# Down product over five PSUM banks, and the S5 matrices loaded where their buffer comes free

## The reference

```python
h = rmsnorm(x, norm_mix);  z = h @ w_in            # 1024 -> 3 x 512: xl, gl, us
hl = rglru(conv(xl));      y_lru = hl * gelu(gl)   # linear recurrence over tokens
ys = s5(us);               g = gelu(ys)            # diagonal complex state space, 32 groups
y_ssm = g * sigmoid(g @ w_glu + b)
x = x + concat(rmsnorm(y_lru), rmsnorm(y_ssm)) @ w_out
h2 = rmsnorm(x, norm_ffn)
ff = silu(h2 @ w_gate) * (h2 @ w_up)               # 1024 -> 2816
x = x + ff @ w_down                                # 2816 -> 1024
y = rmsnorm(x, norm_final)
```

## Time and profile before

| | |
|---|---|
| three runs | 2308.42, 2310.72, 2311.23 us; median 2310.72 |
| the profiled execution | 2311.55 us, of which the span from first to last instruction is 2309.8 |
| TensorE matmul | busy 2214.1 us, 96% of the span, 11582 instructions |
| VectorE, ScalarE, GpSimd | busy 1496.5, 1064.6 and 353.0 us (65%, 46%, 15%) |
| mean granted TensorE clock | 0.985 |
| DMA | 324.52 MB moved, 45.8% share of the 16 engines |

### The profile page before, as it was taken

One profiled execution on the slowest core, in us unless ns is written; L12 is line 12 of the kernel. 1 busy time (PEld: TensorE's weight loads), 2 busy tenths in 40 slices (PEclk: granted clock), 3 DMA queues, 4 the chain that ended last, 5 costly groups with the idle time before them and its releaser, 6 DMA issues.

```text
span 2309.8 us, 30129 instructions
## 1 busy us (share of the span) xinstructions
PE 2214.1 (96%) x11582; PEld 2094.1 (91%) x11582; DVE 1496.5 (65%) x2536; ACT 1064.6 (46%) x1432; POOL 353.0 (15%) x428
## 2 busy tenths in 40 slices
PE   6898889999999999999999999999999999999997
PEld 3565889999999999999999999999999999999996
DVE  8555555687666647875666677666658875665544
ACT  4325532564543455554434664543455464432232
POOL 4022200022101102311110132101102321100001
PEclk8999999999999999999999999999999999999998
DMA  6865233545334454543353655334455643343331
GB/s 209 206 205 158 87 106 118 135 161 170 110 119 148 140 141 160 181 126 120 118 169 119 167 169 172 110 119 148 139 141 160 168 129 111 117 149 110 120 125 60
DMA packets 201759, 324.52 MB, mean 140 GB/s; under 512 B 89296, under 2 KB 132944, under 8 KB 201488
## 3 DMA queue, kind: packets, MB, share of 16 engines
q1 hardware_dynamic: 201488, 322.36, 45.8%
q0 software_dynamic: 128, 0.23, 0.0%
HBM read 298.09 MB, written 26.53 MB: 141 GB/s over the span
## 4 chain that ended last, share of the span: by engine, by line
PE 86%; DVE 7%; ACT 3%; issue 2%; POOL 1%; DMA 1%; SPq 0%; POOLq 0%; DVEq 0%; ACTq 0%
PE acc L920 25%; PE acc L922 25%; PE acc L921 24%; PE acc L993 6%; DVE rstd L1207 1%; POOL tmp L629 1%; PE acc L1024 1%; PE acc L1015 1%; PE acc L1004 1%; PE acc L1014 1%; DVE w_hl L1090 1%; DVE act_hl L1090 1%; PE acc L986 1%; DVE x_acc L1090 0%; DVE s5prod L1090 0%
## 5 line engine op out<-in xcount | busy, mean ns | idle before, releaser
L920 PE MATMUL acc<-act_hl,w_hl 128*128 128x416 f32 x2448 | 877.4, 358 | 10.7 <-DVE act_hl L1090 9.7
L921 PE MATMUL acc<-act_hl,w_hl 128*128 128x416 f32 x2448 | 857.5, 350 | 0.0
L922 PE MATMUL acc<-act_hl,w_hl 128*128 128x416 f32 x2448 | 857.2, 350 | 0.0
L1090 DVE TENSOR_TENSOR w_hl<-w_raw,w_hl 128x1024 fp32r<-128x1024 f32 x416 | 513.4, 1249 | 74.8 <-ACT w_hl L716 73.5
L920 PEld LDWEIGHTS acc<-act_hl,w_hl 128*128 128x128 f32 x2448 | 463.0, 189 | 23.5 <-issue 10.9
L921 PEld LDWEIGHTS acc<-act_hl,w_hl 128*128 128x128 f32 x2448 | 463.7, 189 | 5.7 <-issue 4.8
L922 PEld LDWEIGHTS acc<-act_hl,w_hl 128*128 128x128 f32 x2448 | 462.6, 189 | 2.0
L716 ACT ACTIVATE w_hl<-w_raw 128x1024 fp32r<-128x1024 f32 x416 | 430.5, 1051 | 46.2 <-DMA w_raw<-in_w_ffn 24.1
L1090 DVE TENSOR_TENSOR x_acc<-x_acc,acc 128x416 f32<-128x416 f32 x480 | 272.2, 584 | 196.4 <-PE acc L922 190.0
L920 PE MATMUL acc<-ff_hl,w_hl 128*128 128x416 f32 x880 | 312.6, 355 | 20.2 <-DVE x_acc L1090 17.0
L629 POOL TENSOR_TENSOR tmp<-tmp 128x416 f32<-128x416 f32 x121 | 153.7, 1270 | 1059.9 <-ACT tmp L727 1020.4
(11 more groups left out here) (179 smaller groups left out, 1830.7 us busy)
## 6 DMA issues: line engine op xcount, KB each, us to landing
w_raw<-in_w_ffn SPq DMA_DIRECT2D x330, 512.0 KB, 3.7
w_raw<-in_w_in SPq DMA_DIRECT2D x60, 512.0 KB, 3.5
s5y<-y_dram SPq DMA_DIRECT2D x80, 256.0 KB, 4.2
w_raw<-in_w_out SPq DMA_DIRECT2D x40, 512.0 KB, 3.3
s5t<-t_dram SPq DMA_DIRECT2D x64, 162.0 KB, 3.9
s5v<-v_dram SPq DMA_DIRECT2D x80, 128.0 KB, 3.8
x_acc<-in_x SPq DMA_DIRECT2D x4, 1664.0 KB, 7.6
out_y<-x_acc SPq DMA_DIRECT2D x8, 832.0 KB, 6.6
```

The lines of the kernel that those rows point to most:

```text
L920: pe.matmul(out, w(0), x(0), start=first, stop=False)
L921: pe.matmul(out, w(0), x(1), start=False, stop=False)
L922: return pe.matmul(out, w(1), x(0), start=False, stop=last)
L1090: return v.tensor_tensor(out, x, y, op)
```

## The change

The down product's eight chunks go to fixed banks: 2, 3, 4, GATE, UP, 2, 3, 4. `dn_before` gives the eviction that a chunk has to wait for. The fourth chunk waits besides for the silu of the last gate chunk issued, the fifth for the multiplication of the last up chunk (`gates`); a gate and an up product wait for the eviction of the fourth and the fifth chunk of the last down product (`downs`). SyncE loads V, Y and tables in another order and at other steps: at the start V of three pairs, not two; at ("s5", b, j) first the table of pair gt + 2, then, after the Y product of pair j - 2 of this same step, Y of pair gt + 1, then, after the V product of this same step, V of pair gt + 3.

```diff
+        DN_BANK = (DN, DN + 1, DN + 2, GATE, UP, DN, DN + 1, DN + 2)
+        DN_GATE, DN_UP = DN_BANK.index(GATE), DN_BANK.index(UP)
+
+        def dn_before(n):
+            b, d = n // KD, n % KD
+            used = [m for m in range(d) if DN_BANK[m] == DN_BANK[d]]
+            if used:
+                return b * KD + used[-1] + 1
+            return (b - 1) * KD + max(m for m in range(KD) if DN_BANK[m] == DN_BANK[d]) + 1 if b else 0
...
-                        for gt in range(2):
+                        for gt in range(3):
                             load_v(gt)
-                            load_t(gt)
+                            if gt < 2:
+                                load_t(gt)
...
                 elif kind == "s5":
                     gt = b * GP + j
                     if j < GP and gt + 2 < NB * GP:
-                        if gt >= 1:
-                            n = gt - 1
-                            sp.wait_ge(m_full, USE[("v5", n // GP, n % GP)] + 1)
-                        load_v(gt + 2)
                         if gt >= 2:
                             sp.wait_ge(p_done, gt - 1)
                         load_t(gt + 2)
-                    if j < GP and gt >= 3:
-                        n = gt - 3
-                        sp.wait_ge(m_full, USE[("y5", n // GP, n % GP)] + 1)
-                        load_y(gt)
+                    if j >= 2 and gt + 1 < NB * GP:
+                        sp.wait_ge(m_full, USE[("y5", b, j - 2)] + 1)
+                        load_y(gt + 1)
+                    if j < GP and gt + 3 < NB * GP:
+                        sp.wait_ge(m_full, USE[("v5", b, j)] + 1)
+                        load_v(gt + 3)
...
+            def downs(b, j):
+                return max(0, b * NPAIR - 1 + (j + 1) // 2)
+
+            def gates(m):
+                return min(2 * m + 3, NB * NF)
...
                 elif kind == "gate":
...
+                    if downs(b, j):
+                        pe.wait_ge(dn_free, (downs(b, j) - 1) * KD + DN_GATE + 1)
...
                 elif kind == "up":
...
+                    if downs(b, j):
+                        pe.wait_ge(dn_free, (downs(b, j) - 1) * KD + DN_UP + 1)
...
                     for d in range(4 * j, 4 * j + 4):
                         n = b * KD + d
-                        if n >= 3:
-                            pe.wait_ge(dn_free, n - 2)
-                        out = acc[:, DN + n % 3, 0:tk]
+                        if dn_before(n):
+                            pe.wait_ge(dn_free, dn_before(n))
+                        if d == DN_GATE:
+                            pe.wait_ge(gate_free, gates(b))
+                        elif d == DN_UP:
+                            pe.wait_ge(up_free, gates(b))
+                        out = acc[:, DN_BANK[d], 0:tk]
```

More of the change, by code:

```diff
@@ L1405, in _ @@
                         v.wait_ge(dn_full, n + 1)
-                        tt(x_acc[o][:, d, 0:tk], x_acc[o][:, d, 0:tk], acc[:, DN + n % 3, 0:tk], ADD).then_inc(dn_free, 1)
+                        tt(x_acc[o][:, d, 0:tk], x_acc[o][:, d, 0:tk], acc[:, DN_BANK[d], 0:tk], ADD).then_inc(dn_free, 1)
 def _layout(inp):
```

## The result

| | before | after |
|---|---|---|
| median of the runs beside each other | 2310.97 us (2308.42 to 2314.28, 4 runs) | 2285.14 us (2283.04 to 2287.78, 4 runs) |
| ratio after to before | | 0.9883, 95% interval 0.9871 to 0.9895 |
| the profiled execution | 2311.55 us, span 2309.8 | 2287.78 us, span 2286.0 |
| TensorE matmul busy | 2214.1 us | 2208.6 us |
| mean granted clock | 0.985 | 0.985 |

The kernel is faster, as forecast, but by more: 25.8 us between the medians, 24.0 us between the two profiled executions, where the sum said 20.8. The same program measured again on another occasion gave 2287.64 us (2286.28 to 2288.97, 4 runs) at a ratio of 0.9892 (0.9874 to 0.9910). So the direction and the places held, and the size of the gain was put 3 to 5 us too small; 2285.14 us lies at the lower edge of the range of 2285 to 2300.

A forecast was written before the change was run, and what follows sets the result against it. The prediction took TensorE, its matmuls filling 96% of the span, as the bound, so only its holes and clock could be won: -17.0 + 1.6 - 4.1 - 1.3 = -20.8 us, from 2310.72 to 2289.9 us, range 2285 to 2300.

The forecast's parts named there:

- Term 1: Down product: all 14 TensorE stalls on late evictions go with five banks, -17.0 us.
- none of the 13 is left: Fourth-chunk stalls of the down product: 2.24 us of cover against the largest stall of 1.84 us removes all.
- Term 2: Output product's second chunk, four blocks: 0.4 us each comes back waiting for VectorE's weight remainder, +1.6 us.
- Term 3: S5 Y products: five waits for the landing of Y's matrices go because Y is issued earlier, -4.1 us.
- Term 4: TensorE's clock after 400 us: one of three half-clock stretches goes, -1.3 us; bounds -3.9 to +1.3.
- Steps costed at nothing: 322 more waits on TensorE's queue, gate and up chunks' waits for evictions, SyncE's waits for V products: 0 us.
- A: VectorE bounds the dense stretches, so stalls come back as other waits: -13.7 us, 2297 us, worst 2303; chance 0.15.
- B: The S5 load edit wins nothing, landing only later or "issue" being something else: 2295.3 us; chance 0.07.
- C: The 322 added waits cost TensorE queue time, at 0.1 us each 2322.1 us, slower; chance 0.04.
- D: Banks don't cause the down-product stalls; the sixth chunk would stall as the fourth did: 2306.6 us; chance 0.02.

The follow-up runs named there:

- four banks: The changed kernel with the down product's chunks over four banks (2, 3, 4, GATE, 2, 3, 4, 2) instead of five: 2293.51 us, ratio 0.9922.
- the loads alone: The kernel before with only the new order and steps of the S5 loads, down product still on three banks: 2305.29 us, ratio 0.9974.
- the added waits: The changed kernel with two more, long met waits ahead of each of the 440 down chunks, 880 in all: 2285.81 us, ratio 0.9884.
- only Y: The changed kernel with V and tables loaded as before, only Y's load going out earlier: 2285.94 us, ratio 0.9895.
- the made holes: The changed kernel, fourth and eighth chunks of the last 13 down products also waiting for the eviction of the chunk just before: 2309.86 us, ratio 0.9992.
- the banks alone: The kernel before with only the down product's five banks, S5 loads as before: 2291.23 us, ratio 0.9908.
- the kernel with the late norm: The changed kernel with first hidden chunk's products first, S5 scaling one place earlier, block 1's recurrent-branch norm sums two places later: 2283.10 us, ratio 0.9877.

## Why the prediction was wrong in size

**Term 1 (-17.0) is the step that failed.** It took the drawn idle of 14 stalls for their cost. They cost 20.9 us from start to start. The places, the cause and "none of the 13 is left" were right: the line is empty, and with four banks 0.53 us remain of the one of 1.69, close to what 1.69 - 1.12 says. The numbers that would have mended it were in the text on how to read the profile: 0.35 us is drawn, while the next one starts 0.187 later. A matmul before a hole is drawn 0.16 us past the point where its successor would have started, and the first spacing behind it is 0.30, another 0.11. 14 x 0.28 = 3.9 us. The Trainium skill, "TensorE: Matmul & The Clock Gate", section "Step-by-step: what each phase is for", says that back-to-back matmuls hide the drain of the array and that one standing alone cannot; its section "Single matmul latency" gives a single bf16 matmul a constant of 166 ns at full clock besides the time of its columns. The profile's 0.35 - 0.187 = 0.16 is of that size, but the ends of matmuls are modelled, so no run here shows a drain; what the runs show is the starts. The 0.11 to 0.12 of the spacing behind the hole these sections don't name.

**Term 2 (+1.6) was close:** 2.0 from start to start at the four output products, for the same reason drawn only 0.29 each, where the prediction wanted 0.4. What it did not see is the norm of block 1: 1.3 us given back, 9 and 11 us behind a Y hole that it removed (at 539.50 and 541.72, behind the product at 530.26). It asked of each stall of VectorE's what is late next, but not of the Y holes.

**Term 3 (-4.1)** was sized by drawn idle like term 1, and was 5.3 from start to start; less that 1.3 it is 4.0, and 3.5 in the trace of the loads alone. Right about the cause, the landing; right that V and the tables don't matter.

**Term 4 (-1.3)** came out at 1.55 us, and by luck. There were four stretches, not three, and those that can be laid beside full clock cost 1.55 each, not 1.3: the spacings are 0.35 for 0.187 us, some ten times. The half clock at 1843 went with its hole, and the one at 539 moved to 542.7, behind the new hole, and stayed. One went, the middle that was taken; but with the added waits and with only Y the one at 542.7 is missing behind the same hole, so another execution could have had two or more.

**Steps costed at nothing** held: the added waits, the gate and up chunks' ties to the evictions (no such line among the waits), SyncE's waits.

With 0.28 us more for each of the 14 stalls and the five Y holes (5.3), the same working would have given -20.8 - 5.3 = -26.1, and -24.8 with the 1.3 us of the norm, where 24 to 26 were measured. That rule was read off the two traces after the result, and the made holes tested it.

**The rivals.** A: VectorE bounds only the four holes of 0.29 us. B and C fell by their own experiments. D: the banks alone give 21.4 us behind the 1061st matmul, where both give 23.8.

The remaining 2 us between the profiles' 24 and the medians' 25.8 are not traced: the profiled execution of the changed kernel is the slowest of its four (2287.78), and both profiles reach the 1061st matmul at 320.1 us. Whether the medians of many more runs would end at 24 or at 26 is open.

## What to carry to other kernels

Price a hole by starts, not by drawn idle: from the last start before it to the second start behind it, less two steady spacings; two kernels with the same matmuls show it in TensorE's busy time, together with what half clock adds there. Then ask of every hole that goes, small ones too, which engine TensorE meets next within some 10 us, GpSimd included. A wait that is already met costs TensorE's queue nothing measurable, so a bank may be shared among several users, each with its own wait, as long as the distance to its eviction grows.

## What the runs showed of the hardware

**A hole costs 0.28 us more than is drawn**, with 416 columns in fp32r, at full clock: 26 made holes of 0.68 us cost 0.96 each. Before the Y products, with 52 columns behind the hole, it is 0.20 to 0.24. A wait shorter than 0.16 us is not drawn and still cost 0.24 (1461.47 with four banks).

**880 waits that were met cost less than a run's spread.**

**Half clock stood behind the same hole in one trace and not in another.** Behind the hole of 1.12 us on `tmp` the changed kernel has half clock (at 542.7), and so has its repeat; the kernels with added waits and with only Y have the hole and full clock. Behind the hole of 2.0 us before the last down product it stands in the changed kernel (2259.6) and not with four banks or only Y. No half clock was granted among the 26 made holes of 0.68 us. A stretch of 3.41 us at half clock cost 1.55 us by the starts.

**The start differs between executions.** The 1061st matmul starts between 318.0 and 321.7 us in the thirteen traces, at 320.1 and 321.7 in the two of the changed kernel itself, with half clock at other places. The stretch from 0 to 315 us of the kernel with the late norm, and then of that with more waits, by matmuls done:

```profile
0.00:315.00 315.00, 262.70 (x1026) 178.73 (x1027) 192.86 (x361) 130.98 (x198) 69.13 (x96) 0.92 0.55 168
```

```profile
0.00:315.00 315.00, 265.04 (x1045) 181.69 (x1046) 194.51 (x362) 131.85 (x200) 69.20 (x96) 0.93 0.55 169
```

19 matmuls more in the one, 3.5 us at 0.187. No edit touches that part's order of matmuls. It may be most of the spread of some 4 us within four runs of one kernel, though only one run of each was traced. One profile against another must be compared behind it.
